# Up projections of two MLPs: pairs of column tiles by seven products in place of eight, squares through DRAM

## What is computed

```python
u = jnp.square(jax.nn.relu(h @ w_up[l]))      # (1024,1024) @ (1024,4096)
x = x + rmsnorm(u @ w_down[l], post_mlp_norm[l])
```

## Time and profile before

| | |
|---|---|
| median of three runs | 2883.8 us |
| profiled execution | 2886.94 us, of it span 2885.1 us |
| PE busy | 2772.3 us (96%) |
| DVE, ACT, POOL busy | 1147.7, 810.9, 331.3 us |
| chain that ended last | 87% PE; issue 3%, ACT 4%, DVE 3%, POOL 2% |
| DMA | 158.43 MB on the one queue, 16.8% of 16 engines |

### The profile page before, as it was taken

One profiled execution on the slowest core, in us unless ns is written; L12 is line 12 of the kernel. 1 busy time (PEld: TensorE's weight loads), 2 busy tenths in 40 slices (PEclk: granted clock), 3 DMA queues, 4 the chain that ended last, 5 costly groups with the idle time before them and its releaser, 6 DMA issues.

```text
span 2885.1 us, 31158 instructions
## 1 busy us (share of the span) xinstructions
PE 2772.3 (96%) x12744; PEld 2231.6 (77%) x12744; DVE 1147.7 (40%) x1841; ACT 810.9 (28%) x1360; POOL 331.3 (11%) x290
## 2 busy tenths in 40 slices
PE   6999999999998999999999999989999999999997
PEld 5766688887887788888888778855677888888886
DVE  3223223334436334344344434254464434334345
ACT  4233222223223421221211332365243221221211
POOL 0000000000111210100100110232021110110102
PEclk9999999999999999999999999999999999999999
DMA  3112111112321111111111121000202111111111
GB/s 140 59 66 67 59 44 37 39 42 103 109 95 59 52 51 43 53 50 39 59 44 44 66 93 45 30 16 1 88 22 66 44 51 48 48 52 37 59 44 59
DMA packets 44431, 160.43 MB, mean 56 GB/s; under 512 B 5472, under 2 KB 5728, under 8 KB 44160
## 3 DMA queue, kind: packets, MB, share of 16 engines
q1 hardware_dynamic: 44288, 158.43, 16.8%
HBM read 141.57 MB, written 16.84 MB: 55 GB/s over the span
## 4 chain that ended last, share of the span: by engine, by line
PE 87%; ACT 4%; issue 3%; DVE 3%; POOL 2%; DMA 0%; POOLq 0%; SPq 0%; ACTq 0%; DVEq 0%
PE bank L498 26%; PE bank L500 26%; PE bank L499 26%; PE bank L899 2%; PE bank L631 1%; ACT p L1035 1%; PE bank L558 1%; PE bank L850 1%; PE bank L876 1%; PE bank L675 1%; PE bank L851 0%; PE bank L608 0%; PE bank L877 0%; DVE wlo L1362 0%; POOL accX L1910 0%
## 5 line engine op out<-in xcount | busy, mean ns | idle before, releaser
L498 PE MATMUL bank<-whi,uh 128*128 128x512 f32 x1024 | 406.1, 397 | 5.1 <-DVE ul L1629 5.1
L934 ACT ACTIVATE whi<-raw 128x1024 fp32r<-128x1024 f32 x218 | 225.0, 1050 | 650.3 <-PE bank L500 650.3
L500 PE MATMUL bank<-whi,ul 128*128 128x512 f32 x1024 | 405.5, 396 | 0.0
L499 PE MATMUL bank<-wlo,uh 128*128 128x512 f32 x1024 | 405.5, 396 | 0.0
L1362 DVE TENSOR_TENSOR wlo<-raw,whi 128x1024 fp32r<-128x1024 f32 x218 | 264.3, 1228 | 332.7 <-ACT whi L934 332.7
L1598 DVE TENSOR_TENSOR accX<-bank,accX 128x512 f32<-128x512 f32 x304 | 206.8, 690 | 184.8 <-PE bank L500 184.6
L498 PE MATMUL bank<-hhi,whi 128*128 128x512 f32 x608 | 253.5, 417 | 5.5 <-DVE wlo L1362 3.7
L500 PE MATMUL bank<-hhi,wlo 128*128 128x512 f32 x608 | 240.1, 395 | 0.0
L499 PE MATMUL bank<-hlo,whi 128*128 128x512 f32 x608 | 239.7, 394 | 0.0
L498 PEld LDWEIGHTS bank<-whi,uh 128*128 128x128 f32 x1024 | 193.8, 189 | 50.8 <-DVE ul L1629 5.9
L500 PEld LDWEIGHTS bank<-whi,ul 128*128 128x128 f32 x1024 | 193.7, 189 | 45.4
(11 more groups left out here) (279 smaller groups left out, 4669.8 us busy)
## 6 DMA issues: line engine op xcount, KB each, us to landing
raw<-wp_d SPq DMA_DIRECT2D x218, 512.0 KB, 3.6
gs<-sg_d SPq DMA_DIRECT2D x16, 512.0 KB, 4.0
sg_d<-sig SPq DMA_DIRECT2D x13, 512.0 KB, 2.6
X<-x_d SPq DMA_DIRECT2D x8, 512.0 KB, 8.6
xs<-x_d SPq DMA_DIRECT2D x8, 512.0 KB, 3.3
yd_d<-accX SPq DMA_DIRECT2D x8, 512.0 KB, 2.6
yr<-yd_d SPq DMA_DIRECT2D x8, 512.0 KB, 4.5
out_d<-accX SPq DMA_DIRECT2D x8, 512.0 KB, 2.6
```

Of the source, the lines that this page charges most:

```text
L498: e.matmul(P, sh, mh, start=first, stop=False)
L499: e.matmul(P, sh, ml, start=False, stop=False)
L500: return e.matmul(P, sl, mh, start=False, stop=last)
L934: e.activation(whi[n % SLOTS][:, :], raw[n % RAWS][:, :], ACT.Copy).then_inc(*up("whi", n))
```

## The change

Of the 32 up tiles of each MLP the first NSTD = 6 stay as they were (12 half products). The other 26 are made as NPAIRS = 13 pairs. A pair of tiles, the two halves of k and the two halves of the tokens form a 2x2 by 2x2 product, made with seven products of half the depth (k of 4 tiles, 12 matmuls each) in place of eight (Strassen's scheme in Winograd's form). It needs four sums of h (`T1` to `T4`, 128x4x512 each, once per MLP) and per pair four sums of weights (`s13`, `s24`, 128x1024 each) and five additions at evacuation. The products go to three banks, `a`, `b` and `c`; a later product of the same bank (`n` > 0) adds to what an earlier one left there, after the earlier content has been read out.

Who does what: POOL the weight sums (four operations of 128x512 per pair), the unrounded squares and two of the T sums; DVE the other T sums, all low parts, the additions; ACT the rounding, ReLU and squares. A pair's two pieces come by one transfer of 1 MB into `rawp` (`fetch_pair`), where `raw0` and `raw1` lie. The high and low squares of every up tile now go to a DRAM tensor `ud`, 256 KB each, and are loaded again, 2 MB for each down group, into `ub` (two buffers; `fetch_u`). So all ups run first, then 15 down groups. `T1` and `T2` lie on `acc`, which goes to DRAM (`xd`) ahead of them and is loaded again (`reload`) after the last pair. `row_product` waits for each piece where it is first used. Some semaphores are shared by several topics, and some buffers of the stages around (`xs`, `hj`, `yr`, `lg`, `lb`, `lx`) lie elsewhere; `fetch_x` waits for `wo_end` 1.

In the diff the four parts with `strassen` and `sums_of_h` are, in this order, PE's (`strassen` alone), ACT's (likewise), DVE's and POOL's; the last part is SP's. ACT's `sums_of_h` rounds `T1` (second step), the first weights, `T2` (fifth step), `s13` and `s24` of pair 0, then `T4` (eighth) and `T3` (ninth). Each step of a `sums_of_h` is taken after a half product's evacuation, from the second half of tile 0 on; for tiles 4 and 5 also once ahead of it.

```diff
-NPIECES = 218
+NPIECES = 166
+NSTD = 6
+NPAIRS = 16 - NSTD // 2
...
+def up_order(feed, half_product, name, specs, rest, side):
+    feature_major_start(feed, half_product, name, specs[:4], rest, side)
+    for m in range(4, NSTD):
+        for _ in feature_major(feed, half_product, name, m, specs[m]):
+    next(side, None)
...
-    if t == 0 and c == 0:
-        e.wait_ge(*ok("wlo", ns[-1]))
     if free:
         e.wait_ge(*free)
     for j, k in enumerate(ks_):
+        if t == 0 and c == 0:
+            e.wait_ge(*ok("wlo", ns[j]))
+        if ready and t % 4 == 0 and c == 0:
...
+    def strassen(p):
+        b, banks = p % 2, {}
+        def product(x, n, sh, sl, o, mh, ml):
+            P, free = ring.open("s" + x + tag, p, n, bank=banks.get(x))
+            banks[x] = tally.banks[("s" + x + tag, p, n)]
+            e.wait_ge(*free)
+            for k in range(4):
+                c = slice(o + 128 * k, o + 128 * k + 128)
+                i = mm3(P[:, :], sh[:, c], sl[:, c], mh(k), ml(k), n == 0 and k == 0, k == 3, n > 0)
+            i.then_inc(*ring.full("s" + x + tag, p, n))
+        def part(k1, t1):
+            return (lambda k: hi[:, k1 + k, t1:t1 + 512]), (lambda k: lo[:, k1 + k, t1:t1 + 512])
+        def total(i):
+            return (lambda k: Th[i][:, k, :]), (lambda k: Tl[i][:, k, :])
+        e.wait_ge(*ok("a1l", tag, p))
+        product("a", 0, a1h[b], a1l[b], 0, *part(0, 0))
+        e.wait_ge(*ok("a1l", tag, "s24", p))
+        if p == 0:
+            e.wait_ge(*ok("Tl", tag, 1))
+        product("b", 0, s24h[b], s24l[b], 0, *total(1))
+        product("a", 1, a1h[b], a1l[b], 512, *part(4, 0))
+        e.wait_ge(*ok("a1l", tag, "s13", p))
+        if p == 0:
+            e.wait_ge(*ok("Tl", tag, 2))
+        product("b", 1, s13h[b], s13l[b], 512, *total(2))
+        if p == 0:
+            e.wait_ge(*ok("Tl", tag, 0))
+        product("c", 0, s13h[b], s13l[b], 0, *total(0))
+        e.wait_ge(*ok("a1l", tag, "a22", p))
+        if p == 0:
+            e.wait_ge(*ok("Tl", tag, 3))
+        product("b", 2, a22h[b], a22l[b], 0, *total(3))
+        product("c", 1, s24h[b], s24l[b], 512, *part(4, 512))
+        tally.alias(("pair" + tag, p), ring.latest)
...
+    def squared(name, p, r, h):
+        e.wait_ge(*ok("c" + name, tag, p))
+        if name == "21" or p:
+            e.wait_ge(*ok(*outs(name, p)))
+        e.activation(r[:, :], r[:, :], ACT.Relu).then_inc(*up("relu", tag, name, p))
+        e.wait_ge(*ok("relu", tag, name, p))
+        e.activation(h[:, :], r[:, :], ACT.Square).then_inc(*up("uh", tag, name, p))
+    def strassen(p):
+        more = p + 1 < NPAIRS
+        if p:
+            squared("21", p - 1, r21, h21)
+        if more:
+            weights_a(p + 1)
+        e.wait_ge(*ok("full", "sa" + tag, p, 0))
+        if p:
+            e.wait_ge(*ok("c21", tag, p - 1))
+        else:
+            e.wait_ge(*ok("Ts", tag, "s", 0))
+            e.wait_ge(*ok("Ts", tag, "s", 2))
+        e.activation(p1[:, :], bank_of("sa" + tag, p, 0)[:, :], ACT.Copy).then_inc(*free("sa" + tag, p, 0))
+        if p:
+            squared("12", p - 1, r12[(p - 1) % 2], h12)
+        if more:
+            weights_s13(p + 1)
...
+        e.wait_ge(*ok("full", "sa" + tag, p, 1))
+        e.wait_ge(*ok(*outs("11", p)))
+        e.activation(r11[:, :], bank_of("sa" + tag, p, 1)[:, :], ACT.Relu).then_inc(*free("sa" + tag, p, 1))
+        e.wait_ge(*ok("free", "sa" + tag, p, 1))
...
+    def sums_of_h():
+        T1, T2, _, T4 = (f[:, :, :] for f in fTl)
+        e.wait_ge(*ok("xsp", tag, 7))
+        sum_step(0, part(hi, 0, 512), part(hi, 0, 0), ALU.subtract, "a")
+        yield
+        sum_step(0, T1, fTh[0][:, :, :], ALU.add, "s")
+        yield
+        sum_step(1, part(hi, 4, 512), T1, ALU.subtract, "a")
+        yield
+        sum_step(1, T2, part(lo, 4, 512), ALU.add, "s")
+        yield
+        weights_a(0)
+        weights_a22(0)
+        yield
+        sum_step(3, part(hi, 4, 0), T2, ALU.subtract, "a")
+        yield
+        sum_low(1)
+        yield
+        sum_step(3, T4, part(lo, 4, 0), ALU.add, "s")
+        yield
+        weights_s24(0)
+        weights_s13(0)
+        yield
+        sum_low(0)
+        yield
+        sum_low(2)
+        yield
+        sum_low(3)
...
+    def strassen(p):
+        more = p + 1 < NPAIRS
+        pa, pb, pc = (lambda n, x=x: bank_of("s" + x + tag, p, n)[:, :] for x in "abc")
+        if p:
+            finish_12(p - 1)
+            low("22", l22, f22, h22, p - 1)
+        if more:
+            weights_a(p + 1)
+            weights_a22(p + 1)
+        if p:
+            low("21", l21, f21, h21, p - 1)
+        e.wait_ge(*ok("full", "sb" + tag, p, 0))
+        e.wait_ge(*ok("free", "sa" + tag, p, 0))
+        e.tensor_tensor(out=r12[p % 2][:, :], in0=pb(0), in1=p1[:, :], op=ALU.add).then_inc(*free("sb" + tag, p, 0))
+        if p:
+            low("12", l12, f12, h12, p - 1)
+        if more:
+            weights_s13(p + 1)
+        else:
+            feed.cap = NPIECES
+            feed.ahead(feed.cur + 2)
+        e.wait_ge(*ok("full", "sb" + tag, p, 1))
+        e.tensor_tensor(out=r22[:, :], in0=pb(1), in1=p1[:, :], op=ALU.add).then_inc(*free("sb" + tag, p, 1))
+        low("11", l11, f11, h11, p)
+        if more:
+            weights_s24(p + 1)
+        else:
+            feed.ahead(feed.cur + RAWS)
+        e.wait_ge(*ok("full", "sc" + tag, p, 0))
+        e.wait_ge(*ok("free", "sb" + tag, p, 1))
+        e.tensor_tensor(out=r22[:, :], in0=pc(0), in1=r22[:, :], op=ALU.add).then_inc(*free("sc" + tag, p, 0))
...
+        e.wait_ge(*ok("full", "sb" + tag, p, 2))
+        e.tensor_tensor(out=r21[:, :], in0=pb(2), in1=p1[:, :], op=ALU.add).then_inc(*free("sb" + tag, p, 2))
+    def finish_12(p):
+        r = r12[p % 2]
+        e.wait_ge(*ok("full", "sc" + tag, p, 1))
+        e.wait_ge(*ok("free", "sb" + tag, p, 0))
+        e.tensor_tensor(out=r[:, :], in0=bank_of("sc" + tag, p, 1)[:, :], in1=r[:, :], op=ALU.add).then_inc(*free("sc" + tag, p, 1))
+        tally.alias(("c12", tag, p), ("free", "sc" + tag, p, 1))
...
+    def sums_of_h():
+        T1, T3, t3 = fTh[0][:, :, :], fTl[2][:, :, :], fTh[2][:, :, :]
+        e.wait_ge(*ok("h_" + norm, 7, 1))
+        e.wait_ge(*ok("free", norm, 7, 1))
+        e.wait_ge(*ok("xsp", tag, 7))
+        e.tensor_tensor(out=T1, in0=part(lo, 0, 512), in1=part(lo, 0, 0), op=ALU.subtract).then_inc(*up("Tb", tag, 0))
+        yield
+        weight_sums(0)
+        yield
+        e.tensor_tensor(out=T3, in0=part(hi, 4, 512), in1=part(hi, 0, 512), op=ALU.subtract).then_inc(*up("Tb", tag, "a", 2))
+        yield
+        e.tensor_tensor(out=t3, in0=part(lo, 4, 512), in1=part(lo, 0, 512), op=ALU.subtract).then_inc(*up("Tb", tag, 2))
+        yield
+        e.wait_ge(*ok("Tb", tag, "a", 2))
+        e.wait_ge(*ok("Tb", tag, 2))
+        e.tensor_tensor(out=T3, in0=T3, in1=t3, op=ALU.add).then_inc(*up("Tb", tag, "s", 2))
+        yield
+    def weight_sums(p):
+        b = p % 2
+        s13, s24 = f13[b][:, :], f24[b][:, :]
+        e.wait_ge(*ok("rawp", tag, p))
+        if p == 1:
+            e.wait_ge(*ok("std_end" + tag))
+        elif p > 1:
+            e.wait_ge(*ok("pair" + tag, p - 2))
+        e.tensor_tensor(out=s13[:, 0:512], in0=rawp[:, 1, 0:512], in1=rawp[:, 1, 512:1024], op=ALU.add).then_inc(*up("ws", tag, 1, p))
+        e.tensor_tensor(out=s13[:, 512:1024], in0=rawp[:, 0, 0:512], in1=rawp[:, 1, 0:512], op=ALU.subtract).then_inc(*up("ws", tag, 3, p))
+        e.wait_ge(*ok("ws", tag, 1, p))
+        e.tensor_tensor(out=s24[:, 0:512], in0=s13[:, 0:512], in1=rawp[:, 0, 0:512], op=ALU.subtract).then_inc(*up("ws", tag, 2, p))
+        e.wait_ge(*ok("ws", tag, 2, p))
+        e.tensor_tensor(out=s24[:, 512:1024], in0=rawp[:, 0, 512:1024], in1=s24[:, 0:512], op=ALU.subtract).then_inc(*up("ws", tag, 4, p))
+    def strassen(p):
+        if p:
+            e.wait_ge(*ok("relu", tag, "22", p - 1))
+            square("22", f22, r22, p - 1)
+        if p + 1 < NPAIRS:
+            weight_sums(p + 1)
+        if p:
+            e.wait_ge(*ok("relu", tag, "21", p - 1))
+            square("21", f21, r21, p - 1)
+            e.wait_ge(*ok("relu", tag, "12", p - 1))
+            square("12", f12, r12[(p - 1) % 2], p - 1)
+        e.wait_ge(*ok("free", "sa" + tag, p, 1))
+        square("11", f11, r11, p)
...
+    def fetch_pair(p):
+        if p:
+            e.wait_ge(*ok("a1l", tag, "a22", p - 1))
+            e.wait_ge(*ok("ws", tag, 4, p - 1))
+        else:
+            e.wait_ge(*ok("wlo", first - 1))
+        n = NPIECES + 2 * NPAIRS * i + 2 * p
+        e.dma_start(rawp[:, :, :], wp[n:n + 2].rearrange("n p c -> p n c")).then_inc(*up("rawp", tag, p, by=16))
...
+    def then_pair():
+        yield from rest
+        fetch_pair(0)
+    up_order(feed, half_product, up_name, [std_out(m) for m in range(NSTD)], then_pair(), iter(()))
+    tally.alias(("std_end" + tag,), ("piece", first - 1))
+    fetch_pair(1)
```

(43 more changed lines are left out.)

415 lines of the change are left out of this document (282 added, 133 removed).

## The result

The changed kernel takes 2972.98 us (2970.99 to 2976.03, 4 runs) beside 2884.53 for the kernel before on the same chip (2883.68 to 2886.23, 4 runs): a ratio of 1.0307, 95% interval 1.0289 to 1.0325, so 88.4 us slower. The forecast was 2947 us with a range of 2870 to 2990. The direction and the late r12 addition came as forecast, but the time is 26 us above the forecast (21 by the spans of the two profiled executions). It lies outside the likeliest case's own range of 2915 to 2965, in the one that was given to rival 3. The profiled execution took 2970.99 us with a span of 2969.2, against 2886.94 and 2885.1 before: 84.1 us more.

A forecast was written before the change was run, and what follows sets the result against it. PE bounds the kernel, so time is the number of matmuls. Products -70.7, pairs in the middle +64.7, starts +64, ends +4.9 give +62.9 us on 2883.8: 2947 us, range 2870 to 2990.

The forecast's parts named there:

- the likeliest case: The shared port delays r12 in 22 pairs and the starts of the pairs: 2915 to 2965 us, chance 0.50.
- rival 3: In the pairs PE's clock falls at each wait, 12 us at each end: +98, 2982 us, chance 0.16.
- Products: Up products in the pairs: 84 matmuls in place of 96, 2.72 us less per pair, 26 pairs: -70.7 us.
- One pair in the middle: Pairs 1 to 11 of each MLP: b1 waits 2.24 us for r12, plus 0.7 for the clock: +64.7 us.
- the clock: After b1's wait the clock can fall: 0.4 of 1.7 = 0.7 us per pair, bounds 0 and 1.7.
- The port: POOL's operations and DVE's with two SBUF inputs exclude each other; one that waited runs on 0.14 us shorter than alone.
- Rival 1: The port doesn't bind in the pairs: no wait at b1, 11 us at each start: -44, 2840 us, chance 0.16.
- exclusive lock: The skill's rule between DVE and GpSimd, held whole instructions, read literally: wait about 3.2 us per pair, about 2970 us.
- the row of 2.95 us of idle: Kernel before: after 2.95 us of PE idle, half speed, half product 7.10 us in place of 5.44, 1.66 lost.
- The start: First pair of each MLP: PE waits 30 us for p1, cold start of 1.7: 2 x 32 = +64 us.
- The end: First down groups wait for squares, weights, acc: 5 us per MLP (bounds 1 and 12), old `ul` waits go: +4.9.
- Costed at nothing: Spills, moved buffers, shared semaphores beside 100% PE: nothing; waiting for row pieces one by one hides 1.2 us at most.

The follow-up runs named there:

- experiment 1: Changed kernel with DVE's r12 addition moved ahead of low 21: 2901.28 us, ratio 1.0054.
- experiment 2: Changed kernel with DVE's low parts of a1 and a22 made for 32 columns only from pair 2 on: one run, 2918.35 us.
- experiment 3: Kernel of experiment 1 with, for pair 0 alone, pair 1's roundings and low parts behind p1 and r12: 2896.98 us, ratio 1.0041.
- experiment 5: Kernel of experiment 3 with SP's fetches of pair 1's weights and g3 issued earlier and those of x moved: 2876.55 us, ratio 0.9978.
- experiment 6: Kernel of experiment 5 with low parts of T2 and s24 earlier, T4's behind r12, T3 rounded ahead of T4: 2864.63 us, ratio 0.9928.
- experiment 9: Changed kernel with SP's wait for w_out's second group and the x fetches moved behind that group's raw fetches: 2964.78 us, ratio 1.0274.
- experiment 8: Kernel before with one edit alone, row products wait for their weight pieces one by one: 2879.76 us, ratio 0.9984.

## Why the prediction was right, and where it was off

**Products, -70.7.** 312 matmuls less are there. The time of one was taken from the whole tiles; in pairs without any wait it is 0.2304 us (experiment 1), which takes back 6.8 us. That a matmul of 512 columns takes 0.2267 us everywhere was assumed, and the kernel before shows otherwise: its down products take 0.2324 at the same clock.

**One pair in the middle, +64.7 against 80.4.** The mechanism was right down to the turn: square 12 ahead of low 21, b1 at 10.5 for 10.4. The wait is 2.10 us for 2.24 (46.3 for 49.3 over the 22): r12 is no earlier, but the products ahead of b1 take longer and hide more of it. The term that was mis-sized is the clock: 0.7 us per pair, from a chance of 0.4 that it falls. It falls in 7 of 11 pairs and costs 1.6 there; with the rest of the restart it is 22.69 - 19.35 - 2.10 = 1.24 us per pair, 27.3 for 15.4. So -3.0 for the wait, +11.9 for the clock and +6.8 for the slower matmuls make the 15.7 that were missing. Rival 3, the clock at every wait, was too dark, and the forecast was too bright; the truth lay between, at 2973 for 2947 and 2982. For the same reason the copies of p1 are 21.6 to 23.3 us apart, not 21.3 to 22.

**The port.** Rival 1 is out, by the rows of the pair and by experiment 2. The Trainium skill's exclusive lock ("SBUF — State Buffer", section "Who interferes with whom"), read literally, gave a wait of 3.2 us and 2970 us. The total came near that, but not by this: the measured wait is 2.10 us, by the turns as the rows of before showed them, and what lifts the total to 2973 lies in the clock and in the ends. The 2970 was also too low for its own case. By the prediction's own reading of the row of 2.95 us of idle, a wait of 3.2 us would have cost the clock's 1.7 us each time, which makes 22 x 4.9 = 107.8 us and a time of some 2990 us.

**The start, +64 against 65.3.** a1 of pair 0 was forecast 80.8 us behind the start of the second half and came 81.4 behind it; it was 31.0 and 30.5 us late, plus 2 us at the lower clock. But the profile was expected to show one wait of over 20 us for p1 in each MLP. There are two, 13.7 us for the low part of s24 and then 14 for p1: the chain to the low part of s24 was late too, which the working passed over, and a sum that looks at the last link alone doesn't feel it. Operations of 2048 columns cost 2.28 on DVE and 4.6 on POOL where the other engine is not in the way, as worked out. That the last link was SP's late fetch and the copy of p1 behind it was right too, but experiment 3 shows how little this link alone was worth: 4.3 us, since the next waits stood right behind it. The edits of experiments 5 and 6 behind it took the start from 91.3 to 81.4 us on average.

**The end, +4.9 against 13.0.** The waits for the squares, the fourth weight piece and acc are there (1.5, 3.2 and 3.5 us at most), within the bounds of 1 to 12 for each MLP. What was not in the sum is the gain row g3: its fetch is queued behind the transfers of squares, DVE waits 3.50 us for it at 1676.01 and PE 3.00 behind that. Issued one wait earlier it saves some 4 us (experiment 5).

**Costed at nothing.** "The spills, moved buffers and shared semaphores lie beside 100% PE: nothing": the moved buffers of x need a wait for the second group of w_out, and that wait stands on SP ahead of the next weight fetches. It cost some 4.8 us (experiment 9). The prediction asked what waits for the moved transfer, and not what is queued behind its new wait. And waiting for row pieces one by one was held to hide 1.2 us at most, at one place; it hid 1.6 and 2.3 us at two others (experiment 8). The two errors nearly cancel. The -7.2 us between the MLPs is for the larger part luck: the clock fell less often in this stretch than in the profile of before.

Breaking even was put at a wait of 0.1 us per pair with these starts. Experiment 1, with no wait in the pairs at all, is 0.54% slower than before: the slower matmuls and the ends.
